# A two-layer hybrid backbone on one core: mixer channels numbered by halves, first modulation loaded in two column halves

## The reference

```python
mod = silu(cond) @ w_ada[l] + b_ada[l]
sh1, sc1, g1, sh2, sc2, g2 = split(mod, 6)
out, k, v, h_fin = token_mixer(x * (1 + sc1) + sh1, ...)
x = layer_norm(ALPHA * x + g1 * out, ln_g[l, 0], ln_b[l, 0])
ff = hier_moe(x * (1 + sc2) + sh2, ...)
x = layer_norm(ALPHA * x + g2 * ff, ln_g[l, 1], ln_b[l, 1])
```

## Time and profile before

| | |
|---|---|
| median of 3 runs | 1266.91 us (1265.58 to 1268.49) |
| profiled execution | 1266.91 us, its span 1265.1 us |
| mean granted TensorE clock | 0.976 of full |
| PE busy | 1200.8 us, 95% of the span |
| DVE busy | 963.9 us, 76% |
| ACT busy | 720.1 us, 57% |
| DMA | 358.83 MB, mean 284 GB/s |

### The profile page before, as it was taken

One profiled execution on the slowest core, in us unless ns is written; L12 is line 12 of the kernel. 1 busy time (PEld: TensorE's weight loads), 2 busy tenths in 40 slices (PEclk: granted clock), 3 DMA queues, 4 the chain that ended last, 5 costly groups with the idle time before them and its releaser, 6 DMA issues.

```text
span 1265.1 us, 15747 instructions
## 1 busy us (share of the span) xinstructions
PE 1200.8 (95%) x5950; PEld 940.7 (74%) x5953; DVE 963.9 (76%) x1151; ACT 720.1 (57%) x692; POOL 74.6 (6%) x121
## 2 busy tenths in 40 slices
PE   4989999999999999999989999999998999999994
PEld 0767777877677888888857777777777888888883
DVE  0745657787689889888877475758858998888887
ACT  1543544553567777677754355445436776777773
POOL 0401000101000000000020010010000000000000
PEclk8999998999999999999999999989999999999997
DMA  9988863637899999999957877444449999999980
GB/s 356 301 288 304 304 225 118 199 134 295 320 356 357 389 366 355 354 361 342 362 137 251 316 254 278 167 141 168 165 157 336 382 384 360 356 345 363 347 317 34
DMA packets 99490, 358.83 MB, mean 284 GB/s; under 512 B 9188, under 2 KB 12736, under 8 KB 83024
## 3 DMA queue, kind: packets, MB, share of 16 engines
q1 hardware_dynamic: 87504, 295.12, 63.8%
q0 software_dynamic: 11904, 62.63, 14.1%
HBM read 352.92 MB, written 5.83 MB: 284 GB/s over the span
## 4 chain that ended last, share of the span: by engine, by line
PE 70%; DVE 13%; ACT 5%; DMA 5%; issue 3%; DVEq 3%; ACTq 1%; SPq 0%; POOL 0%; POOLq 0%
PE bank L955 66%; DVE wl L1874 4%; PE bank L958 4%; ACT wh L1561 2%; DMA first<-in_w_ada 2%; DMA raw<-in_w_in 1%; DMA adaw<-in_w_ada 1%; DVE merged L1874 1%; DVEq L2227 1%; DVE seg L2351 1%; DVE tmp L2211 1%; DVE tmp L1874 1%; DMA decay<-decay_rows 1%; DVE xbc L2146 0%; DVE xbc L2143 0%
## 5 line engine op out<-in xcount | busy, mean ns | idle before, releaser
L1874 DVE TENSOR_TENSOR wl<-raw,wh 128x2048 fp32r<-128x2048 f32 (+1 forms) x268 | 607.2, 2275 | 114.3 <-ACT wh L1561 60.7
L1779 ACT ACTIVATE wh<-raw 128x2048 fp32r<-128x2048 f32 x192 | 367.4, 1915 | 51.1 <-PE bank L955 36.0
L955 PE MATMUL bank<-wh,xgh 128*128 128x512 f32 x512 | 209.9, 410 | 0.0
L955 PE MATMUL bank<-wh,xgl 128*128 128x512 f32 x512 | 203.6, 398 | 0.0
L1561 ACT ACTIVATE wh<-raw 128x2048 fp32r<-128x2048 f32 (+1 forms) x76 | 142.3, 1873 | 69.9 <-PE bank L955 49.7
L955 PE MATMUL bank<-wl,xgh 128*128 128x512 f32 x512 | 140.4, 395 | 0.0
L955 PE MATMUL bank<-wh,hTh 128*128 128x512 f32 x448 | 129.8, 412 | 0.9 <-ACT hTh L1590 0.5
L955 PE MATMUL bank<-wh,hTl 128*128 128x512 f32 x448 | 123.2, 396 | 0.5 <-DVE hTl L1874 0.5
L955 PE MATMUL bank<-wl,hTh 128*128 128x512 f32 x448 | 122.8, 395 | 0.2 <-DVE wl L1874 0.2
L955 PEld LDWEIGHTS bank<-wl,xgh 128*128 128x128 f32 x512 | 96.1, 188 | 23.5 <-DVE wl L1874 0.2
L955 PEld LDWEIGHTS bank<-wh,xgl 128*128 128x128 f32 x512 | 97.0, 190 | 20.3
(11 more groups left out here) (301 smaller groups left out, 1391.0 us busy)
## 6 DMA issues: line engine op xcount, KB each, us to landing
raw<-in_moe_w SPq DMA_DIRECT2D x256, 512.0 KB, 5.2
raw<-in_moe_w SPq DMA_DIRECT2D x64, 1024.0 KB, 6.4
raw<-in_w_in SPq DMA_DIRECT2D x52, 1024.0 KB, 6.0
adaw<-in_w_ada POOLq DMA_DIRECT2D x32, 1024.0 KB, 6.6
raw<-in_w_branch SPq DMA_DIRECT2D x12, 1024.0 KB, 5.3
raw<-in_w_ada SPq DMA_DIRECT2D x8, 1024.0 KB, 9.8
raw<-in_w_o SPq DMA_DIRECT2D x8, 1024.0 KB, 4.9
first<-in_w_ada SPq DMA_DIRECT2D x4, 1024.0 KB, 17.5
```

Of the source, the lines that this page charges most:

```text
L955: return behind(nc.tensor.matmul(*args, **kw))
L1779: tally(A_(wh[c][:, :], slot[r], ACT.Copy), part_high[c])
L1874: return V.tensor_tensor(o, a, b, op)
```

## The change

1. **Channels of the mixer's input** are numbered `(h p c)`: half h holds channels 512h to 512h+511. Loads of `w_in`, of the two bias rows and of the layer-norm rows, and the turns of x, follow.
2. **First modulation by halves.** The columns of `w_ada` for half 0 of shift and scale come first: four slots of `raw`, each with two chunks of 2 x 512 columns, in two DMAs of 512 KB each. Half 1 goes to `first0` to `first3` after q, x and k of half 0, partly after v of half 0. `accumulate_half`, `take_half` and `modulation_half` do one half each. POOL issues 12 small bias and norm loads instead of 3.
3. **Order of q, k, v** in both layers: half 0 of q, k (stream 0, then stream 1), then v, then half 1 of q, k, v. In layer 0 PE accumulates the second modulation half around v of half 0 and turns it inside v of stream 1. v's banks are 5 and 6.
4. **Between mixer and experts**: the last two pieces of `next_ada` come after `rank`; in layer 1 `keep_busy` 5 stands there. The `SELECTED` gather of group 0 moves into `up(0)`. ACT takes layer 1's modulation row (`take_row`) later, after the second gather.

```diff
@@ layer_pieces
-    out += halves("q", "k", "v") + [("ws",)]
+    out += [(w, h) for h in range(2) for w in "qkv"] + [("ws",)]
@@ make_plan
+    for s in range(2):
+        plan.append((f"v{s}", 5 + s))
@@ sync
-                w = lay(A["w_in"], l).rearrange("(p c) n -> p c n", c=DC)
+                w = lay(A["w_in"], l).rearrange("(h p c) n -> h p c n", h=2, c=4)
...
+            def load_columns(h, i, tile, done):
+                w = lay(A["w_ada"], 0).rearrange("(p c) n -> p c n", c=DC)
+                for a in range(2):
+                    src = w[:, 2 * i + a, 0:PIECE].rearrange("p (v h n) -> p v h n", v=2, h=2)[:, :, h, :]
+                    sp.dma_start(tile[:, a * 1024:(a + 1) * 1024].rearrange("p (v n) -> p v n", v=2), src).then_inc(done, 16)
 
             for i in range(SLOTS):
-                load(0, i)
-            load_first(0)
-            load_first(1)
+                load_columns(0, i, raw[:, i, :], slot_full[i])
             sp.dma_start(cst[:, :], A["consts"]).then_inc(once, 16)
-            load_first(2)
-            load_first(3)
             load(0, SLOTS)
             sp.dma_start(x[:, 0, :], A["x_prompt"][0]).then_inc(x_in[0], 16)
             sp.dma_start(x[:, 1, :], A["x_sample"][0]).then_inc(x_in[1], 16)
+            load(0, SLOTS + 1)
+            for i in range(2):
+                load_columns(1, i, first[i], first_in[i])
+            load(0, SLOTS + 2)
+            for i in range(2, 4):
+                load_columns(1, i, first[i], first_in[i])
@@ tensor
+            def accumulate_half(h, pieces):
+
+                name = ("ada0", "ada0b")[h]
+                t = bank_free(pe, 0, name) if pieces[0] == 0 else bank[USE[0][name][0]]
+                for i in pieces:
...
+                    wv = w.rearrange("k (a v p c) -> k a v p c", a=2, v=2, p=P)
+                    for a in range(2):
+                        for v in range(2):
+                            r = 32 * (2 * v + h)
+                            ins = mm(t[r:r + 32, :].rearrange("k (p c) -> k p c", p=P), cT[:, 2 * i + a, :], wv[:, a, v],
+                                     start=i == 0 and a == 0, stop=i == 3 and a == 1)
...
+                for s in range(2):
+                    for w in "qk":
+                        project_half(l, (w, 0), 0, [f"{w}0", f"{w}1"], (s,))
+                        if s == 0 and w == "q":
+                            turn_x(l, "x1T", (1,))
+                if l == 0:
+                    accumulate_half(1, range(2))
+                project_half(l, ("v", 0), 0, ["v0", "v1"], (0,))
+                if l == 0:
+                    accumulate_half(1, range(2, 4))
+                project_half(l, ("v", 0), 0, ["v0", "v1"], (1,), (lambda: turn_mod(0, 0, "adaT0b")) if l == 0 else None)
+                for w in "qkv":
+                    project_half(l, (w, 1), 1, [f"{w}0", f"{w}1"])
...
-                next_ada(6, 8)
                 pe.wait_ge(s0_act, 3 * l + 3)
...
+                next_ada(6, 8)
+                if l == L - 1:
+                    keep_busy(l, "busy5", 5)
...
+                                if i == 0 and h == 1 and c == 2:
+                                    gather(tally, rnd, 0, SELECTED)
@@ scalar
+            def take_half(h):
+
+                name = ("ada0", "ada0b")[h]
+                t = bank_full(act, 0, name)
+                if h:
+                    act.wait_ge(half_turned, 1)
+                for v in range(2):
+                    r = slice(32 * (2 * v + h), 32 * (2 * v + h) + 32)
+                    ins = A_(ada_row[r, :].rearrange("k (c p) -> k p c", c=DC // 2), t[r, :].rearrange("k (p c) -> k p c", c=DC // 2), ACT.Copy)
...
@@ vector
+                    rows("x1T", 0)
+                    convert_to(l, 1)
+                    low(2)
+                    convert_to(l, 2)
+                    modulation_half(1)
+                    low(3)
+                    low(4)
```

More of the change, by code:

```diff
@@ L807, in hybrid_backbone @@
         N_PARAM = 10
+        N_BADA = 6 * L
         @block.gpsimd
@@ L1145, in _ @@
             pe.wait_ge(c_ready, 1)
-            for key in ada(0, 0):
-                accumulate(0, "ada0", key)
+            accumulate_half(0, range(4))
             pe.wait_ge(once, 16)
@@ L1518, in stream @@
                                 turn_mod(l, 0, "adaT_next")
-                            gather(tally, rnd, 0, SELECTED)
                         if i:
@@ L1604, in modulate @@
                     between()
+                    if l == 0 and n == 0:
+                        for s in range(2):
+                            t = bank_full(act, l, f"x1T{s}1")
+                            frees(A_(merged[:, s, NW:D], t[:, :], ACT.Copy), f"x1T{s}1")
+                        bank_emptied(act, l, "x1T10")
+                        high(1, 0, 4)
+                        convert_to(l, 2)
+                        take_half(1)
+                        act.wait_ge(mod_ready, 1)
+                        for s in range(2):
+                            for c in range(4, DC):
+                                A_(merged[:, s, c * P:(c + 1) * P], merged[:, s, c * P:(c + 1) * P], ACT.Identity,
+                                   bias=shift_[:, s, c:c + 1], scale=gain[:, s, c:c + 1])
+                            act.drain().then_inc((s0_act, s1_act)[s], 1)
+                            high(s, 4, 8)
+                        return
                     rows(0, 1)
                     act.drain().then_inc(s0_act, 1)
-                    high(0, 4, 8)
+                    if n:
+                        rows(1, 1)
+                        act.drain().then_inc(s1_act, 1)
+                        return
+                    bank_emptied(act, l, "x1T10")
+                    high(1, 0, 4)
                     rows(1, 1)
                     act.drain().then_inc(s1_act, 1)
-                    if n == 0:
-                        bank_emptied(act, l, f"{which}10")
-                    high(1, 0, 4)
+                    high(0, 4, 8)
                     high(1, 4, 8)
+                    convert_to(l, 2)
                 def take(name, dst, func, done, width=512, shape=None):
@@ L1821, in stream @@
                     gathered(0, 1)
+                    if rnd == 0 and l < L - 1:
+                        take_row(l, 0, "ada_next")
                     piece(2)
@@ L2090, in _ @@
                 if l == 0:
-                    modulation(l, 0, "adaT0")
+                    modulation_half(0)
                     convert_to(0, 0)
```

123 lines of the change are left out of this document (83 added, 40 removed).

## The result

The changed kernel took 1271.51 us in the median of 20 runs, the kernel before 1267.2 in as many: a ratio of **1.0037** (95% interval 1.0024 to 1.0051), which is slower by 4.7 us where +1.3 was forecast. One run of each lay far out (1288.53 us, in the slow state, and 4098.88 us) and is not in the ratio. The profiled execution took 1271.17 us, its span is 1269.4, against 1265.1 before. Most of the chain of reasons held; the sizes that did not hold are mostly those of TensorE's clock.

A forecast was written before the change was run, and what follows sets the result against it. PE, busy 95% of the span, was taken to bound the kernel, with loads bounding its start. Terms 4.2 - 2.8 - 0.4 + 0.3 = +1.3 us on 1266.91 gave 1268.2 us, range 1263.0 to 1272.5.

The forecast's parts named there:

- A: Start of layer 0: with less loaded ahead of x, q begins at 28.6 us, 8.8 us earlier.
- B: Layer 0, among v's matmuls: accumulating and turning the second modulation half is no longer hidden in load waits, +8.0 us.
- the rival of cheap accumulation: Second half's accumulation in layer 0: rounds of two groups overlap, 3.5 us less, 1264.7 or down to 1262.7 us; chance 0.22.
- C(1) to C(3): Layer 0 start: new PE waits, 1.6 us for k's `wl1`, 1.45 at the second modulation's turn, 5.2 before q of half 1.
- C(4): Layer 0, q of half 1: `wl0` 0.5 us late and half clock after the 5 us wait, together 1.2 us.
- D: Layer 0, v's end to z: 3.5 us in place of 5.95, z at full clock; -3.7 us in all.
- A to D: Layer 0 up to z: -8.8 + 8.0 + 8.7 - 3.7 = +4.2 us.
- E: Router and first experts of layer 0: moved accumulations and the earlier `SELECTED` gather gain 2.8 us, between 1.6 and 3.3.
- The rival of the clock: At layer 0's router the moved work does not keep the clock up, so 0.7 us of gain is missing; chance 0.28.
- F: Layer 1: router gains 0.4 us from the clock; its start costs 0.3 (nothing to 0.5) for v's banks and k's rope.
- The first rival: Clock falls longer after the wait before q of half 1 and stays low at the routers: 1270.6 us; chance 0.28.
- The third rival: Start of layer 0: half-megabyte transfers take 2.5 us each, x lands no earlier, the gain is gone: 1277 us; chance 0.03.

The follow-up runs named there:

- Experiment 1: Changed kernel with ACT's conversions of q and k of half 1 (DVE likewise) ahead of the second modulation in layer 0: 1263.76 us, 0.9953; repeated 1265.98 us, 0.9982.
- experiment 3: Changed kernel with 20 matmuls of constants filling PE's wait before q of half 1 in layer 0: 1273.64 us, 1.0046 of the kernel before.
- experiment 2: Changed kernel with 10 matmuls of constants in PE's wait before q of half 1 in layer 0: 1271.87 us, 1.0025 of the kernel before.
- experiment 4: Changed kernel with the first modulation whole again, both halves loaded and accumulated ahead of q: 1271.13 us, 1.0024 of the kernel before.
- experiments 3 and 8: experiment 3; and the changed kernel with earlier conversions and k's low part, plus matmuls of constants before the second turn and small turns: 1268.5 us, 1.0005.

## Why the prediction came out as it did

The time lay inside the range, and 3.3 us above the forecast; the forecast was no difference that could be told, and a slowdown came that can be. At z of layer 1 the profile was 8.3 us behind the kernel before, 6.6 more than the terms give, and 3.7 us came back behind it, for the most part from a slow stretch that the kernel before had there. That is in no term, so a time this near was in part luck. Term by term:

- **A held.** q at 28.6 was forecast, 28.54 came, 8.9 us earlier. Its parts were off in both directions: the last `w_ada` half was in use at 16.98 (16.4 forecast), x landed at 22.3 (issued at 12.5, 9.8 us; 21.7 forecast), the accumulation did not run at half speed (1.91 us for a piece, where 3.5 was taken) and was done at 18.9, and x was turned at 22.31 (23.7), ahead of the modulation all the same. The row of 1.94 us from which half speed was read lies where the granted clock is 1.00, so the clock did not explain it; what did is open.
- **B held.** Two pieces of halves (2 MB) between v's matmuls took 3.56 us (43.71 to 47.27), or 1.78 for a megabyte as worked out, so two empty partition groups of four save nothing; the rival of cheap accumulation falls.
- **C(1) to C(3) held.** Beyond PE's own pace of 0.93 us for a group, k's low group came 1.47 us late (1.6), the turn 1.38 (1.45), q of half 1 5.26 (5.2). Experiment 1 shows that the wait of C(3) comes from the order of work on ACT and not from a need of the data.
- **C(4) failed, the first step that did.** It had 1.2 us, 0.5 of them for `wl0`, so 0.7 for the clock, less than the 1.3 that the prediction itself read behind the shorter wait of 3.35 us. `wl0` cost nothing and the clock 2.2: the three groups behind the wait take 4.99 us from start to start where three take 2.80. Slow groups follow in all eight profiles in which PE idled 2.9 us or more between v of half 0 and z of layer 0; in experiment 3, with the wait filled, they go. So the idle time is their cause, as far as one filled execution can show it; experiment 2 shows that half of it filled does not prevent them.
- **A term is missing: the clock at q's start.** From 28.54 to 32.69 three groups took 4.15 us instead of 2.80, 1.35 lost. The kernel before begins q at full speed in its profile, but with the router edits alone, which come long after, its first group took 1.91 us instead of 1.17; and five of the twelve profiles of kernels with the new order begin it at full speed or nearly. So this belongs to an execution and not to the edit. With it and C(4), v was over at 83.25 instead of 80.7.
- **D held.** v's end to z took 3.69 us (3.5), at the full clock. Its reason, that z's weights and ACT come in time, is what experiment 4 shows from the other side: there v ended early and ACT, held by a load, did not.
- **A to D** came to +8.25 at the start of z, or +7.1 from its third group on, where the slow z of before is counted in (81.82 before, 88.89 after); +4.2 was forecast. From there to the router another 0.9 were lost, in no term; this execution has a slow stretch at 144 that the kernel before has not.
- **E failed in the profile, not in the mechanism.** 2.8 us were forecast; 3.0 came where the clock holds, and 1.55 in the two profiles of the changed kernel, since the 16 turns took 3.58 and 3.4 us. The rival of the clock had priced this at 0.7; it is 1.5.
- **F held for the router and failed for layer 1's start.** The router of layer 1 gained 0.34 us (0.4): from its second turn of x to the first turned `hid` less the shift, +4.57 to +4.23. Layer 1's start cost 1.9 instead of 0.3 in this execution: the copy of v 0.78, the turns' wait on DVE 1.31 and slow groups. In the second profile the same piece cost 0.6. Behind it the 3.7 us came back.

The first rival named the mechanism and the condition (a wait over 4 us; slow for over 3 us) and its time, 1270.6, is the nearest. Its part for F did not come (0.34 us were gained there). It should have been the forecast: the row for a slow restart after an idle 3.35 us was in hand, and the wait worked out was half again as long. The third rival falls with A: x was turned at 22.31. It was also what the Trainium skill, "DMA: Bandwidth & Descriptors", would have, in its rule on batching to a megabyte (section "Bandwidth"). The prediction held 421 GB/s against it, a rate from before its half-megabyte transfers moved; while they did, the kernel before had 392 (25 to 30 us). The loads of half a megabyte ran at 312 GB/s from 10 to 15 us where whole ones had 421, and at 396 from 15 to 20 (columns as above, the last is GB/s):

```profile
10.00:15.00 5.00, 3.29 (x14) 0.67 (x14) 0.00 (x0) 0.00 (x0) 0.26 (x1) 1.00 1.11 312
15.00:20.00 5.00, 3.12 (x14) 0.49 (x10) 0.73 (x3) 1.05 (x2) 0.00 (x0) 1.00 1.05 396
```

The first stretch also carried the added bias loads, so the rule's part in it is not separated; it was far from the doubling. (The prediction's step to a doubling was loose besides: 2 us beside the 1.25 us that half a megabyte takes at 421 GB/s would be more than that.)

Open: why the slow stretches fall where they do, and why a place goes slow in one execution and not in the next. No run here controls them beyond the filled waits of experiments 3 and 8, and neither lowered the time.

## What to carry to other kernels

When a transfer is split to begin earlier, follow the consumer's queue behind the second part: here the gain at the start was real, but the accumulation that had been hidden in load waits cost most of it, and an in-order ACT queue with three conversions standing behind rows that came late cost the rest and more. Moving the conversions ahead in two queues took back 0.6 to 0.8%, and brought the kernel from 0.4% behind the kernel before to level with it or 0.5% ahead. Price an added wait at its length and the slow matmuls behind it, some 2 us after 5 us idle, and ask of a lead which load it will run into next. And compare two orders by repeated, side-by-side timing: one profile of each can differ by 6 us with no edit between them.

## What the hardware showed that was not expected

- The same instructions gave spans of 1269.4 and 1275.4 us, and 1264.0 and 1258.2, with PE's busy time 7.8 and 5.2 us apart and DVE's and ACT's within 0.5. The slow stretches that make this up come at recurring places, one of them, between 644 and 660 us, in all fourteen profiles; which of the others come varies from one execution to the next. The Trainium skill, "TensorE: Matmul & The Clock Gate", Part 1, says that how many matmuls run slow at a kernel's start varies between runs of one kernel, and advises not to fit a count. The trace agrees as far as it goes (q's first group took 2.04 us in one profile of the changed kernel and 1.74 in the other), and shows the same later in the kernel; here the variation is as large as the effect of the change.
- A wait of 5.09 us was followed by 2.2 us of loss. Filled with 4.26 us of other matmuls it was followed by none (one profile); filled with 2.10 us, by groups of 1.72 and 1.91 us.
- Modulating four chunks from SBUF took ACT 1.63 to 1.65 us, where the same from the matmul banks took 1.48.
- A copy of 32 partitions took ACT as long as one of 128: 2.06 us for two, against 1.04 for one.
